# A two-layer hybrid block in one kernel: gate products with the weights as stationary side, rotation on VectorE, and another order at the start of the last attention

## The reference

```
# odd layer (gated linear attention)
q, k, v, r, lr = split(rmsnorm(x) @ w_in)
z = einsum('bsdr,drk->dbsk', lr.reshape(B, S, 2, 16), w_gate_lr) + b_gate
log_alpha = log_sigmoid(z) / 16

# last attention
proj = rmsnorm(x) @ w_in                   # 16 heads x 64 of q, then 48 gate columns
q = rope(rmsnorm_per_head(q, q_norm))      # rotates dims 0..7 with 8..15 of each head
gates = sigmoid(proj[..., 1024:])          # 3 branches x 16 heads
out = (gates[0] * compressed(q) + gates[1] * selected(q) + gates[2] * window(q)) @ w_out
```

## Time and profile before

| | us |
|---|---|
| median of 3 runs (2817.19 to 2821.1) | 2819.29 |
| the profiled execution | 2819.6 |
| its span, first to last instruction | 2817.7 |
| PE busy, 13128 matmul records | 2735.3 |
| DVE / ACT / POOL busy | 1362.6 / 698.9 / 1638.6 |
| mean granted clock of PE | 0.988 |

### The profile page before, as it was taken

The page is one execution under the profiler, slowest core; times in us unless marked ns, Lnnn a source line. Parts: engine busy times, 40 slices in busy tenths (PEclk is TensorE's granted clock), DMA queues, the critical chain, the costliest instruction groups (busy, mean ns, idle before and its releaser), DMA issues. The chain is left out here.

```text
span 2817.7 us, 35952 instructions
## 1 busy us (share of the span) xinstructions
PE 2735.3 (97%) x13128; PEld 2180.9 (77%) x13128; DVE 1362.6 (48%) x1588; ACT 698.9 (25%) x1190; POOL 1638.6 (58%) x952
## 2 busy tenths in 40 slices
PE   7999989988999999989999999999999999999999
PEld 5777777756788888856888888788888766788887
DVE  8787824573531452056541346642246477643142
ACT  3434422243210110075210011310012277311010
POOL 4666755504565665601666566566566598566565
PEclk9999999999999999999999999999999899999999
DMA  4222222202232222200332232333232100123232
GB/s 176 93 87 92 95 90 82 75 9 74 83 112 82 97 97 91 97 15 16 97 104 91 95 105 82 127 97 112 82 104 90 53 2 2 63 95 116 79 100 86
DMA packets 62026, 235.63 MB, mean 84 GB/s; under 512 B 6880, under 2 KB 7008, under 8 KB 61792
## 3 DMA queue, kind: packets, MB, share of 16 engines
q1 hardware_dynamic: 61920, 234.21, 25.3%
HBM read 232.08 MB, written 2.10 MB: 83 GB/s over the span
## 5 line engine op out<-in xcount | busy, mean ns | idle before, releaser
L313 POOL TENSOR_TENSOR w_lo<-ring,w_hi 128x1024 fp32r<-128x1024 f32 (+2 forms) x388 | 1003.8, 2587 | 57.7 <-issue 4.6
L311 POOL CAST w_hi<-ring 128x1024 fp32r<-128x1024 f32 (+2 forms) x388 | 444.1, 1144 | 965.9 <-PE ps L331 767.0
L329 PE MATMUL ps<-hi,w_hi 128*128 128x512 f32 x2064 | 810.4, 393 | 8.5 <-POOL w_lo L313 4.4
L331 PE MATMUL ps<-hi,w_lo 128*128 128x512 f32 x2064 | 804.3, 390 | 0.0
L330 PE MATMUL ps<-lo,w_hi 128*128 128x512 f32 x2064 | 804.2, 390 | 0.0
L329 PEld LDWEIGHTS ps<-hi,w_hi 128*128 128x128 f32 x2064 | 388.2, 188 | 98.0 <-POOL w_lo L313 6.9
L330 PEld LDWEIGHTS ps<-lo,w_hi 128*128 128x128 f32 x2064 | 388.4, 188 | 81.6 <-issue 2.2
L331 PEld LDWEIGHTS ps<-hi,w_lo 128*128 128x128 f32 x2064 | 388.0, 188 | 81.0
L329 PE MATMUL ps<-hid_hi,w_hi 128*128 128x512 f32 x704 | 274.3, 390 | 0.0
L330 PE MATMUL ps<-hid_lo,w_hi 128*128 128x512 f32 x704 | 273.9, 389 | 0.0
L331 PE MATMUL ps<-hid_hi,w_lo 128*128 128x512 f32 x704 | 273.9, 389 | 0.0
(11 more groups left out here) (311 smaller groups left out, 3389.5 us busy)
## 6 DMA issues: line engine op xcount, KB each, us to landing
ring<-in_ffn_in SPq DMA_DIRECT2D x176, 512.0 KB, 3.5
ring<-in_even_in SPq DMA_DIRECT2D x48, 512.0 KB, 4.3
ring<-in_ffn_out SPq DMA_DIRECT2D x32, 768.0 KB, 4.2
ring<-in_ffn_out SPq DMA_DIRECT2D x32, 640.0 KB, 3.8
ring<-in_even_out SPq DMA_DIRECT2D x16, 512.0 KB, 3.5
ring<-in_odd_v SPq DMA_DIRECT2D x8, 512.0 KB, 3.5
ring<-in_odd_r SPq DMA_DIRECT2D x8, 512.0 KB, 3.5
ring<-in_odd_qk SPq DMA_DIRECT2D x8, 512.0 KB, 3.6
```

What stands on the lines that cost most here:

```text
L311: nc.gpsimd.tensor_copy(high[:, j % 2, 0:cols], ring[:, j, 0:cols])
L313: nc.gpsimd.tensor_tensor(low[:, j % 2, 0:cols], ring[:, j, 0:cols], high[:, j % 2, 0:cols].bitcast(F32), ALU.subtract).then_inc(sem["w_re ...
L329: nc.tensor.matmul(bank, w_hi[:, j % 2, w], x_hi[:, k, :], start=(start and k == 0), stop=False)
L331: mm = nc.tensor.matmul(bank, w_lo[:, j % 2, w], x_hi[:, k, :], start=False, stop=(stop and k == kt - 1))
```

## The change

- `lr`: 24 matmuls in two-part form (`w_lr_hi`, `w_lr_lo` against `hi`, `lo`) instead of eight in plain float32. ACT and DVE then split the result in two parts too; with the gate weights split and stacked in 96 rows (high x high, high x low, low x high), `gla_gates` is one pass per matmul.
- The 48 gate columns: the weights (high part in rows 0 to 47, low part in rows 64 to 111 of the output) are the stationary side, `hi` and `lo` stream past with 512 columns, 16 matmuls behind tile 2; ACT copies the result out, four small float32 matmuls behind tile 3 turn it to tokens on partitions and add the two halves, and the sigmoid follows behind tile 3's copies.
- The rotation: the order of the features in a head is changed (`KEY_ORDER`, in queries and keys alike) so that the partners lie 32 rows apart; `q_shift` multiplies four groups of 8 rows by the signed sines and writes them 32 rows away. No `rot` matmul is left.
- The scales of the head norms come in two halves (`q_root`, `q_scales`), by Ln and Exp; the first half behind tile 4.
- Order: scores(0) and scores(1) stand ahead of query tile 7 on PE, with maxima, probs and scale of these steps ahead of tile 7's work on ACT and POOL; tile 7's shifts, its sum and the second half of the scales are spread over turns 1 to 6 of DVE's loop. The probabilities of steps 0 and 1 lie elsewhere (`pr_of`), as `lo` is still read.
- POOL splits one slot of `nsa_out` ahead of the softmax instead of two.

```diff
@@ -470,17 +475,27 @@
+        Q_BANK = [0, 1, 2, 3, 0, 1, 4, 6]
+        def pr_of(s, e):
+            return prt[:, 1, e, :] if s == 0 else (root, acc)[e] if s == 1 else pr[:, s % 4, e, :]
...
@@ -618,23 +633,25 @@
-                mm = nc.tensor.matmul(ps[0:32, 4, :], w_lr[:, k * 32:(k + 1) * 32], res[:, k, :],
-                                      start=(k == 0), stop=(k == DT - 1))
+                c = slice(k * 32, (k + 1) * 32)
+                nc.tensor.matmul(ps[0:32, 4, :], w_lr_hi[:, c], hi[:, k, :], start=(k == 0), stop=False)
+                nc.tensor.matmul(ps[0:32, 4, :], w_lr_hi[:, c], lo[:, k, :], start=False, stop=False)
+                mm = nc.tensor.matmul(ps[0:32, 4, :], w_lr_lo[:, c], hi[:, k, :], start=False, stop=(k == DT - 1))
-            w_gate = con("w_gate_lr").rearrange("p (h d c) -> p h d c", h=GLA_HEADS, d=2)
+            w_gate = w_gate_r[:, :].rearrange("p (h d c) -> p h d c", h=GLA_HEADS, d=2)
-                    pe.wait_ge(sem["lr_copied"], 1)
+                    pe.wait_ge(sem["lr_ready"], 1)
-                    mm = nc.tensor.matmul(ps[:, 6 + d, :], w_gate[0:32, h, d, :], lr_t[0:32, :], start=True, stop=True)
+                    mm = nc.tensor.matmul(ps[:, 6 + d, :], w_gate[0:96, h, d, :], lr_t[0:96, :], start=True, stop=True)
...
@@ -988,41 +1005,48 @@
-            def q_turn(m):
+            def q_norms(m):
-                if m >= 2:
-                    pe.wait_ge(sem["q_rotated"], m - 1)
-                nc.tensor.matmul(ps[:, 4 + m % 2, :], con("rot"), gq[:, m % 2, :], start=True, stop=True)\
-                    .then_inc(sem["q_turned"], 1)
+                if m == 4:
+                    pe.wait_ge(sem["norms_read"], 1)
-            for m in range(DT):
-                j = m % RING
-                if m >= RING:
-                    pe.wait_ge(sem["q_copied"], m - RING + 1)
+            def gate_products():
+                pe.wait_ge(sem["weights_gained"], 2)
+                for k in range(DT):
+                    nc.tensor.matmul(ps[0:GATE_ROWS, 5, :], w_gates[:, k, :], hi[:, k, :], start=(k == 0), stop=False,
+                                     skip_group_check=True)
+                    mm = nc.tensor.matmul(ps[0:48, 5, :], w_gates[:, k, 0:48], lo[:, k, :], start=False,
+                                          stop=(k == DT - 1), skip_group_check=True)
+                mm.then_inc(sem["gates_mm"], 1)
+            def gate_turns():
+                pe.wait_ge(sem["gates_copied"], 1)
+                for t in range(TT):
+                    mm = nc.tensor.matmul(ps[:, 4, t * 48:(t + 1) * 48], gate_rows[:, t * P:(t + 1) * P],
+                                          gate_halves[0:GATE_ROWS, :], start=True, stop=True)
+                mm.then_inc(sem["gates_turned"], 1)
+            def q_tile(m):
+                if m in (4, 5):
+                    pe.wait_ge(sem["q_shifted"], m - 3)
+                if m == 6:
+                    pe.wait_ge(sem["gates_taken"], 1)
+                if m == 7:
+                    sums_read(pe, "mix_1")
-                product(ps[:, j, :], j, DT, hi, lo, tile_ready if m == 0 else None)
-                if m == 0:
-                    sums_pe(pe, "mix_1")
-                if m > 0:
-                    q_turn(m - 1)
-            sums_read(pe, "mix_1")
-            pe.wait_ge(sem["weights_gained"], 2)
-            for t in range(TT):
-                for k in range(DT):
-                    mm = nc.tensor.matmul(ps[:, 6, t * 48:(t + 1) * 48], res[:, k, t * P:(t + 1) * P],
-                                          w_gates[:, k * 48:(k + 1) * 48], start=(k == 0), stop=(k == DT - 1))
-            mm.then_inc(sem["gates_mm"], 1)
-            q_turn(DT - 1)
+                product(ps[:, Q_BANK[m], :], m % RING, DT, hi, lo, tile_ready if m == 0 else None)
+                if s == 0:
+                    pe.wait_ge(sem["q_shifted"], 6)
...
@@ -1085,10 +1113,26 @@
-            for it in range(-2, NSA_STEPS + 2):
+            for m in range(DT - 1):
+                q_tile(m)
+                if m == 0:
+                    sums_pe(pe, "mix_1")
+                if m > 0:
+                    q_norms(m - 1)
+                if m == 2:
+                    gate_products()
+                if m == 3:
+                    gate_turns()
+            nsa_scores(0)
+            nsa_scores(1)
+            q_tile(DT - 1)
+            q_norms(DT - 2)
+            nsa_scores(2)
+            q_norms(DT - 1)
+            for it in range(1, NSA_STEPS + 2):
-                if 0 <= it - 1 < NSA_STEPS:
+                if it - 1 < NSA_STEPS:
...
@@ -1205,6 +1249,10 @@
+            act.wait_ge(sem["lr_copied"], 1)
+            for rows in (0, 64):
+                a = nc.scalar.activation(lr_t[rows:rows + 32, :], lr_f[0:32, :], ACT.Copy)
+            a.then_inc(sem["lr_high"], 1)
...
@@ -1392,24 +1440,40 @@
-            for m in range(DT):
-                j = m % RING
+            def q_copy(m):
-                nc.scalar.activation(gq[:, m % 2, :], ps[:, j, :], ACT.Identity, scale=con("q_norm"))
-                nc.scalar.activation(sq_q[:, m % 2, :], ps[:, j, :], ACT.Square).then_inc(sem["q_copied"], 1)
+                nc.scalar.activation(gq[:, m % 2, :], ps[:, Q_BANK[m], :], ACT.Identity, scale=con("q_norm"))
+                nc.scalar.activation(sq_q[:, m % 2, :], ps[:, Q_BANK[m], :], ACT.Square).then_inc(sem["q_copied"], 1)
+            def q_root(n):
+                act.wait_ge(sem["norms_mm"], 4 * n + 4)
+                for t in range(TT):
+                    op = nc.scalar.activation(ssq[:, t, 8 * n:8 * n + 8], ps[:, 7, t * 16 + 8 * n:t * 16 + 8 * n + 8], ACT.Ln,
+                                              bias=eps, scale=rtok2[:, t:t + 1])
+                op.then_inc(sem["norms_read"], 1)
+                act.drain()
+                nc.scalar.activation(rq[:, :, 8 * n:8 * n + 8], ssq[:, :, 8 * n:8 * n + 8], ACT.Exp, scale=-0.5)\
+                    .then_inc(sem["norm_root"], 1)
+            for m in range(DT - 1):
+                q_copy(m)
-            act.wait_ge(sem["norm_scale"], 1)
-            act.wait_ge(sem["gates_mm"], 1)
-            for t in range(TT):
-                nc.scalar.activation(gts[:, t, :], ps[:, 6, t * 48:(t + 1) * 48], ACT.Sigmoid, scale=rtok[:, t:t + 1])
-            act.wait_ge(sem["norms_mm"], DT)
-            for t in range(TT):
-                nc.scalar.activation(ssq[:, t, :], ps[:, 7, t * 16:(t + 1) * 16], ACT.Sqrt, bias=eps, scale=rtok2[:, t:t + 1])
-            act.drain().then_inc(sem["norm_root"], 1)
+                if m == 2:
+                    act.wait_ge(sem["gates_mm"], 1)
+                    nc.scalar.activation(gate_rows, ps[0:GATE_ROWS, 5, :], ACT.Copy).then_inc(sem["gates_copied"], 1)
+                if m == 3:
+                    act.wait_ge(sem["norm_scale"], 1)
+                    act.wait_ge(sem["gates_turned"], 1)
+                    for t in range(TT):
+                        op = nc.scalar.activation(gts[:, t, :], ps[:, 4, t * 48:(t + 1) * 48], ACT.Sigmoid, scale=rtok[:, t:t + 1])
+                    op.then_inc(sem["gates_taken"], 1)
+                if m == 4:
+                    act.preload_act_table_set(LOG_SET)
+                    q_root(0)
...
@@ -1437,8 +1501,13 @@
-            for it in range(-2, NSA_STEPS + 3):
-                if 0 <= it - 1 < NSA_STEPS:
+            nsa_probs(0)
+            nsa_probs(1)
+            q_copy(DT - 1)
+            nsa_probs(2)
+            q_root(1)
+            for it in range(1, NSA_STEPS + 3):
+                if it - 1 < NSA_STEPS:
...
@@ -1626,17 +1695,23 @@
-            for k in range(DT):
-                op = V.tensor_scalar(w_lr[:, k * 32:(k + 1) * 32], con("w_lr")[:, k * 32:(k + 1) * 32],
-                                     con("g_odd_pre")[:, k:k + 1], None, ALU.mult)
-            op.then_inc(sem["weights_gained"], 1)
+            V.tensor_copy(w_lr_hi[:, :], con("w_lr"))
+            dve.drain()
+            V.tensor_tensor(w_lr_lo[:, :], con("w_lr"), w_lr_hi[:, :].bitcast(F32), ALU.subtract).then_inc(sem["weights_gained"], 1)
+            gate = con("w_gate_lr")
+            V.tensor_copy(gate_hi[64:96, :], gate[64:96, :])
+            V.tensor_copy(w_gate_r[0:64, :], gate[0:64, :])
+            dve.drain()
+            V.tensor_tensor(w_gate_r[64:96, :], gate[64:96, :], gate_hi[64:96, :].bitcast(F32), ALU.subtract)
-            V.tensor_tensor(lr_t[0:32, :], ps[0:32, 4, :], rinv[0:32, :], ALU.mult).then_inc(sem["lr_copied"], 1)
+            V.tensor_tensor(lr_f[0:32, :], ps[0:32, 4, :], rinv[0:32, :], ALU.mult).then_inc(sem["lr_copied"], 1)
+            dve.wait_ge(sem["lr_high"], 1)
+            V.tensor_tensor(lr_t[32:64, :], lr_f[0:32, :], lr_t[0:32, :].bitcast(F32), ALU.subtract).then_inc(sem["lr_ready"], 1)
...
@@ -1951,29 +2026,51 @@
-            for k in range(DT):
-                op = V.tensor_scalar(w_gates[:, k * 48:(k + 1) * 48], con("w_gates")[:, k * 48:(k + 1) * 48],
```

(76 more changed lines are left out.)

73 lines of the change are left out of this document (46 added, 27 removed).

## The result

The changed kernel takes 2801.79 us (median of four executions, 2796.54 to 2802.66) against 2820.19 for the kernel before (four, 2817.19 to 2824.23): ratio 0.9929, 95% interval 0.9914 to 0.9944. Six more executions later had a median of 2798.36, ratio 0.9925 (0.9909 to 0.9941). All ten together have a median of 2799.97, so the change is worth 18 to 22 us. The profiled execution took 2796.54 (span 2794.7), 23.1 less than the profiled one of before; the forecast, 24.2 less, was made against that one. So there are two things to explain: where the 23 went, and why most executions of after are slower than its profiled one.

A forecast was written before the change was run, and what follows sets the result against it. PE, busy 97% of the span, was taken as the bound. Linear attention -6.0, last attention up to scores(9) -18.7 and +0.5 behind it sum to -24.2 from 2819.6: 2795.4, stated as 2795.0, range 2789.5 to 2803.

The forecast's parts named there:

- Linear attention, -6.0: Linear attention: lr saves 1.5 us, gates of heads 0 to 2 save 4.5; together -6.0, bounds 0 and -6.5.
- Head 3's saving: Linear attention's gate pair for head 3: the freed 1.5 us become a wait ahead of L715, saving nothing.
- E, +0.35: Moment PE leaves query tile 6, last attention: five rotations gone (-4.3), gate work added (+4.65); 2218.66 instead of 2218.31.
- From E on: Last attention from PE leaving tile 6 to scores(9): scores(9) start at 2253.2 instead of 2271.92, -18.7 us.
- idle ahead of norms(7): PE, last attention: norms of tile 7 wait 2.2 us for ACT's copy of tile 7 behind probs(1).
- rival 2: Last attention: DVE's sum gets between POOL's cast and subtraction, norms(7) come 2.1 us earlier; 2793 to 2794, chance 0.10.
- scores(9) at E + 34.5: Last attention: scores(9) start 34.5 us after PE leaves tile 6; 30.35 without any wait.
- rival 1: Start of last attention: clock falls in PE's new idle, losing 1.7 us, up to 4; 2797 to 2799, chance 0.20.
- waits for POOL: PE ahead of scores(9): turn(2) waits 0.7 us, turn(3) 0.5, turn(4) 0.3 for POOL's scaling.
- the likeliest case: The whole kernel: the forecast itself, 2795.0 us, with chance 0.45.
- After scores(9), +0.5: Steady rhythm behind scores(9): as before, POOL late, DVE's added steps with about 1 us slack per turn; 0.5 us added.
- rivals 3, 4 and 5: Swallowed linear-attention gain, 2801, 0.08; tile 7 hiding nothing, 2799, 0.10; clock falling at 48-column matmuls, 2828, 0.02.

The follow-up runs named there:

- gla_only: The kernel before with only the linear attention's part of the change; 2812.44 us, ratio 0.9978.
- rot_kept: The changed kernel with PE's part of the old rotation put back as a dummy matmul ahead of each tile's norm sums; 2807.05 us, ratio 0.9937.
- port_gap: The changed kernel with VectorE's 32 short additions at 1741 us, outside the change, drained after every fourth; 2795.98 us, ratio 0.9912.
- after_again: The changed kernel unaltered, run again for a second profile and more times; 2798.36 us.
- gates_streamed: The changed kernel with the 64 old plain f32 gate matmuls behind query tile 3 in place of the new gate products and turning; 2808.55 us, ratio 0.9963.
- order_undone: The changed kernel with query tile 7 whole ahead of the first scores again, as before the change; 2801.08 us.
- idle_filled: The changed kernel with tile 6's norm sums repeated three times as filler in PE's idle ahead of tile 7's norms; 2801.4 us.

## Why the prediction was right, and where it was not

- *Linear attention, -6.0:* gla_only -6.5 in its stretch, -6.2 in the whole; in after's profile, with other falls of the clock, the table has -5.4. lr took 5.55 us in 24 matmuls (5.5 forecast), 0.23 each as in the product's row, so it was right to keep the row. Head 3's saving did become a wait, 1.35 us at L732 (before none). `lr_ready` cost nothing; the DVE work ahead of odd_r neither.
- *E, +0.35 (2218.66 against 2218.31):* from the token sums of mix_1, 42.86 against 42.63, +0.2. rot_kept confirms 0.86 for each rotation.
- *From E on:* maxima(0) forecast at E + 7.0, measured 6.9; copy of tile 7 done at 13.6, 13.8; idle ahead of norms(7) 2.2, 2.38. DVE's sum was held by POOL's subtraction as told from the earlier trace rows, and rival 2 did not come about.
- *The failed term is scores(9) at E + 34.5:* measured 36.8. The missing 2.3 us are the clock, rival 1, which I had at 0.20: PE works 5.5 us at 1.2 GHz, which costs 2.7, while its waits for POOL are 0.6 us in all (0.19 and 0.44) and not the 1.5 forecast. The mistake was in the reading of the earlier trace rows: the 1.4 us of idle in one window and the 1.6 in the other belong to two waits of the same length, 2.01 us, which the windows' edges cut. The timeline of before has both:

```profile
612.60 1.09 PE L715 MATMUL ps<-consts,arena 128*128 128x128 f32 x8 [2.01 <-ACT arena L1259]
...
632.44 1.70 PE L715 MATMUL ps<-consts,arena 128*128 128x128 f32 x8 [2.01 <-ACT arena L1259]
```

  No fall behind the first, one behind the second: the trace of before already said that 2 us of idle can go either way. The wait of 2.38 us had a fall with it in all four profiles that have it (the fall comes 1.0 us into it in after and port_gap, 2.1 in after_again, and 1.2 us behind its end in gates_streamed), while the earlier of the two waits of 2.01 us (at about 602 in after) had no fall behind it in five of the fourteen profiles. So the likeliest case should have carried the fall: 2797.5.
- *After scores(9), +0.5:* +1.0 in both profiles of after; most of it is one wait of PE for POOL, 15.7 us behind scores(9), of 1.02 us instead of 0.26. That the late DVE steps cause it isn't shown: order_undone, which has none of them, is at +0.4, and port_gap, which has them all, at +0.5.
- *The change's gain, -16.6 in the stretch,* splits by single undoings into new order 5.9, gates 6.4, rotation 4.25. That they sum to 16.6 is luck: each contains its own share of the clock (3.4 us more lost than after in order_undone and in gates_streamed, 3.4 less in rot_kept), and these shares don't add up to the 8.5 that the whole change gains. I had explained the gates by their length alone at either clock; about half of the 16.6 us is the clock.
- *Median against profile:* forecast -24.2; the profiled pair shows -23.1, the medians -18 to -22. The misses in the profile are +2.1 in the stretch, +0.6 in linear attention and +0.5 behind scores(9), less the 1.9 ahead of the change: that they cancel to about 1 us is luck. The rest is probably the blocked cast, in seven of ten profiles, which neither profile that I compared contains. Whether before is hit as often stays open: its own profile and gla_only's are free of it, and its unprofiled executions (2814 to 2828) don't say.
- The range, 2789.5 to 2803, holds the result; rivals 3, 4 and 5 didn't occur.

## What to carry to other kernels

Narrow matmuls cost twice: they take PE's time and, in three kernels here (before, gates_streamed, idle_filled), the clock fell under them; exchange the sides where that makes them wide, and don't fill a wait with them. When PE's wait is ended by a copy, follow that engine's queue back to what stood ahead of it: here the first link was a weight split on POOL that nobody needed yet, and behind each link removed was the next one. Read how long a wait is from the timeline, not from the idle share of a window that may cut it in two. Before you trust a few microseconds between two medians, compare the same stretch in two profiles: here an unrelated collision at 1744 us moved whole executions by 5.
